# S5's angle fractions on GpSimd instead of VectorE, and another order of VectorE's steps at the end of bc's first half

## What is computed

```
lam_bar = jnp.exp(lam * dt)
bu = jnp.einsum("gpc,blgc->blgp", b_bar, ug.astype(jnp.complex64))
_, states = lax.associative_scan(_lin_rec, (a_el, bu), axis=1)
y = jnp.einsum("gcp,blgp->blgc", cmat, states).real + d_skip * ug
```

## Time and profile before

| | before |
|---|---|
| time, median of 3 runs | 1672.93 us (1672.84 to 1673.79) |
| the profiled execution: time, span | 1673.03 us, 1671.3 us |
| PE busy | 1661.6 us (99%) |
| DVE busy | 1315.7 us (79%) |
| ACT busy | 984.2 us (59%) |
| POOL busy | 234.9 us (14%) |
| granted clock of PE, mean | 0.999 |

### The profile page before, as it was taken

The page is one execution under the profiler, slowest core; times in us unless marked ns, Lnnn a source line. Parts: engine busy times, 40 slices in busy tenths (PEclk is TensorE's granted clock), DMA queues, the critical chain, the costliest instruction groups (busy, mean ns, idle before and its releaser), DMA issues.

```text
span 1671.3 us, 24189 instructions
## 1 busy us (share of the span) xinstructions
PE 1661.6 (99%) x8216; PEld 1386.3 (83%) x8216; DVE 1315.7 (79%) x1723; ACT 984.2 (59%) x1365; POOL 234.9 (14%) x337
## 2 busy tenths in 40 slices
PE   9999999999999999999999999999999999999998
PEld 8888888888888888888888888888888888888886
DVE  7999999999999996545766868888878888845544
ACT  7676676666677877444547754444444454454554
POOL 7843342221111110000000200000000000000001
PEclk9999999999999999999999999999999999999999
DMA  7666766666857666666787577777777777766564
GB/s 255 214 196 197 207 202 202 191 196 180 248 201 252 218 223 205 197 192 208 243 254 223 176 233 241 237 245 243 243 244 242 243 233 243 232 190 198 191 189 127
DMA packets 182873, 361.61 MB, mean 216 GB/s; under 512 B 17520, under 2 KB 45456, under 8 KB 182672
## 3 DMA queue, kind: packets, MB, share of 16 engines
q1 hardware_dynamic: 169264, 340.23, 64.0%
q0 software_dynamic: 12336, 19.92, 5.1%
q10 hardware_dynamic: 1200, 0.53, 0.1%
HBM read 335.41 MB, written 18.92 MB: 212 GB/s over the span
## 4 chain that ended last, share of the span: by engine, by line
PE 74%; DVE 2%; ACT 1%; issue 0%; DVEq 0%
PE psum L1930 23%; PE psum L1931 23%; PE psum L1932 23%; PE psum L1915 2%; PE psum L1917 1%; PE psum L2051 1%; DVE wlo L1216 1%; PE psum L2052 0%; DVE dec L1566 0%; ACT whi L740 0%; PE psum L2058 0%; PE psum L1966 0%; DVE dec L1562 0%; ACT xtok L949 0%; DVE zx L1629 0%
## 5 line engine op out<-in xcount | busy, mean ns | idle before, releaser
L740 ACT ACTIVATE whi<-raw 128x1024 fp32r<-128x1024 f32 x580 | 612.6, 1058 | 583.2 <-PE psum L1932 472.0
L1216 DVE TENSOR_TENSOR wlo<-raw,whi 128x1024 fp32r<-128x1024 f32 x580 | 708.8, 1228 | 312.6 <-ACT whi L740 305.9
L1915 PE MATMUL psum<-act,whi 128*128 128x512 f32 x1088 | 342.5, 396 | 0.0
L1930 PE MATMUL psum<-whi,nw 128*128 128x512 f32 x704 | 274.1, 389 | 0.0
L1931 PE MATMUL psum<-wlo,nw 128*128 128x512 f32 x704 | 273.9, 389 | 0.0
L1932 PE MATMUL psum<-whi,nw 128*128 128x512 f32 x704 | 273.9, 389 | 0.0
L1917 PEld LDWEIGHTS psum<-act,wlo 128*128 128x128 f32 x1088 | 204.4, 188 | 48.3
L1917 PE MATMUL psum<-act,wlo 128*128 128x256 f32 x1088 | 213.7, 278 | 0.0
L1915 PEld LDWEIGHTS psum<-act,whi 128*128 128x128 f32 x1088 | 165.6, 189 | 3.3 <-issue 3.2
L1932 PEld LDWEIGHTS psum<-whi,nw 128*128 128x128 f32 x704 | 132.1, 188 | 27.6
L1930 PEld LDWEIGHTS psum<-whi,nw 128*128 128x128 f32 x704 | 132.1, 188 | 27.3
(11 more groups left out here) (255 smaller groups left out, 2236.7 us busy)
## 6 DMA issues: line engine op xcount, KB each, us to landing
raw<-in_w_up SPq DMA_DIRECT2D x176, 512.0 KB, 4.8
raw<-in_w_zx SPq DMA_DIRECT2D x96, 512.0 KB, 3.7
raw<-in_w_down SPq DMA_DIRECT2D x88, 512.0 KB, 4.3
raw<-in_w_gate SPq DMA_DIRECT2D x64, 512.0 KB, 5.2
raw<-in_w_proj SPq DMA_DIRECT2D x48, 512.0 KB, 4.4
raw<-in_w_bc SPq DMA_DIRECT2D x32, 512.0 KB, 3.9
raw<-in_w_glu SPq DMA_DIRECT2D x32, 512.0 KB, 4.5
raw<-in_w_out SPq DMA_DIRECT2D x32, 512.0 KB, 4.7
```

What stands on the lines that cost most here:

```text
L740: fn(whi[:, s, :], raw[:, s, :], ACTF.Copy).then_inc(hi_ready, 1)
L1216: V.tensor_tensor(wlo[:, s, :], raw[:, s, :], whi[:, s, :], ALU.subtract).then_inc(lo_ready, 1)
L1915: mm(psum[:, b + t, :], whi[:, s, cols(t)], x, start=first, stop=False)
L1930: mm(banks[:, t, :], x_hi, high[:, k], start=first and k == 0, stop=False)
```

## The change

In blocks 1 to 7 POOL makes the fractions, with two instructions each (TENSOR_SCALAR, TENSOR_TENSOR) and a wait between them. DVE keeps those of block 0 (`if start`). POOL's other steps in these turns are put in order around them: the filling of output weights is first in a turn, the first fraction stands ahead of `load_next`, the folds and the step sizes (now `dt_rows`) stand behind the second fraction, and the last fraction of a turn, that of the next block's tile 0, behind the third state sum.

In the last group of bc's first half DVE's order becomes: scan, turn on, the group's sums, the state sum, and then the third low part, which stood between the scan and the turn on.

```diff
             horner_steps((11, 9))
             state_sums(0)
-            fill_next(0)
-            load_next(1)
-            fold(2, 2)
-            state_sums(1)
-            fill_next(1)
-            load_next(2)
-            fold(4, 4)
-            state_sums(2)
-            fill_next(2)
-            load_next(3)
-            horner_steps((7, 5, 3))
...
-            state_sums(3)
-            fill_next(3)
-            for blk in range(4, 7):
-                load_next(blk)
-                state_sums(blk)
-                fill_next(blk)
-            state_sums(7)
+
+            def fractions(count):
+
+                pool.wait_ge(angm_ready, count)
+                step.done(G.tensor_scalar(angm[:, 1, :], angm[:, 0, :], MAGIC, None, ALU.subtract))
+                G.tensor_tensor(ang[:, 0, :], angm[:, 1, :], ang[:, 0, :], ALU.subtract).then_inc(ang_ready, 1)
+
+            def dt_rows():
+
+                horner_steps((7, 5, 3))
...
+            for blk in range(1, 8):
+                fill_next(blk - 1)
+                fractions(blk * 4 + 2)
+                if blk < 7:
+                    load_next(blk)
+                state_sum(blk, 0)
+                fractions(blk * 4 + 3)
+                if blk in (1, 2):
+                    fold(2 * blk, 2 * blk)
+                if blk == 3:
+                    dt_rows()
+                state_sum(blk, 1)
+                fractions(blk * 4 + 4)
+                state_sum(blk, 2)
+                if blk < 7:
+                    fractions(blk * 4 + 5)
             pool.wait_ge(rot_free, 1)
...
                     group_conv(*before)
+                    ends_first_half = name == "bc" and i == 0 and r == per - 1
                     s5_scan(tile, last)
-                    if not last:
+                    if not last and not ends_first_half:
                         lo(2)
                     cpad_free(*before)
                     s5_turn_on(r)
-                    if r == per - 1 and name == "bc":
+                    if last:
                         last_state_sum(blk)
                     if r == per - 1 and not last:
                         group_sums(name, i, r)
-                    if not last:
+                    if ends_first_half:
+                        last_state_sum(blk)
+                        lo(2)
+                    if start:
                         s5_fractions(blk * 4 + (r + 2))
                     if r == per - 1 and name == "zx":
                         last_state_sum(blk)
```

More of the change, by code:

```diff
@@ L646, in _ @@
             state_sums(0)
-            fill_next(0)
-            load_next(1)
-            fold(2, 2)
-            state_sums(1)
-            fill_next(1)
-            load_next(2)
-            fold(4, 4)
-            state_sums(2)
-            fill_next(2)
-            load_next(3)
-            horner_steps((7, 5, 3))
-            step.done(G.tensor_scalar(series, series, 1.0, 2.0, ALU.add, ALU.mult))
-            mul(series, series, ratio)
-            step.done(G.tensor_scalar(square, dtx[0:DT, :], 0.0, None, ALU.max))
@@ L672, in _ @@
-            state_sums(7)
+            def fractions(count):
[4 more added lines that the diff above has]
+                horner_steps((7, 5, 3))
+                step.done(G.tensor_scalar(series, series, 1.0, 2.0, ALU.add, ALU.mult))
+                mul(series, series, ratio)
+                step.done(G.tensor_scalar(square, dtx[0:DT, :], 0.0, None, ALU.max))
+                mul(dt, series, square, ALU.add)
+                G.tensor_scalar(ratio, dt, dtp[0:DT, 2:3], -1.0, ALU.mult, ALU.mult).then_inc(dt_row, 1)
+                pool.wait_ge(dt_row, 1)
+                for k, at_k in ((0, 0), (1, P)):
+                    pool.dma_start(scr[:, at_k:at_k + P], dtw[64 * k:64 * k + HEADS, 0, :]).then_inc(scr_w, 16)
```

## The result

| | before | after |
|---|---|---|
| time, median | 1673.04 us (1672.63 to 1674.09) | 1675.82 us (1675.5 to 1676.54) |
| ratio, 95% interval | | 1.0016 (1.0010 to 1.0022) |
| the profiled execution: span | 1671.3 us | 1674.5 us |

The changed kernel takes 2.78 us more. The time lies inside the prediction's range, but the forecast change of 1.41 us is half of the measured one. The interval of the ratio lies above 1, and the shortest time after (1675.5 us) lies above the longest before (1674.09), so the kernel is slower, by 0.16%. The 3.35 us that the prediction took for the least that can be told from no change were too coarse a measure.

What follows compares the result with a forecast made beforehand. PE bounds the kernel, with DVE's gapless bc queue just behind: 7 x 0.52 - 6 x 0.33 = 1.66 us, less the lead of 0.25, gives 1.41 us more, a median of 1674.3 us; range 1672.4 to 1676.6.

Steps and rivals of the forecast that it cites:

- What bounds the kernel: Mixer: PE sets the pace; DVE is just ahead in zx turns, behind in bc, where its gains and losses add up.
- the lead of 0.25 us: Late in bc's second half: DVE has a low part ready at most 0.25 us before PE begins its unit at 425.98.
- Removed from DVE: bc, 344.30 to 424.53: six fractions of 0.33 us leave DVE's queue, 1.98 us in all.
- The price on DVE: POOL's pair beside DVE's SBUF instructions: 0.42 + 0.10 = 0.52 us a fraction, seven fractions in bc.
- The upper bound of 0.84: Most that one POOL fraction could cost DVE: 2 x 0.42 = 0.84 us.
- The signs: bc: DVE's steps and low parts 0.1 to 0.42 us longer, tiles about 0.2; PE's late low-part waits 1 to 2 us.
- Rival (b): DVE stands still for POOL's whole instruction: 1.61 us a fraction, 1682 us; chance 0.09, including any price above 0.8.
- Rival (a): DVE and POOL hardly meet: 0.25 us or less a fraction, PE's 0.41 wait gone, 1672.5 us; chance 0.27.
- POOL's queue at nothing: POOL's queue, blocks 1 to 7: some 1.8 us a tile fits in POOL's room and costs nothing.
- the spare 1.2 us: Block 3, the tightest place: POOL's fraction done at 235.3, ACT reads it at 236.56.
- The end of bc's first half: New order could remove PE's 0.41 us wait, but DVE is 1.09 us later, so most of this gain goes again.
- The zx turns: 0.76 us a turn falls into DVE's 2.5 us of slack and costs nothing.

Runs made afterwards that it cites:

- experiment 3: Changed kernel with the fractions of blocks 1 to 7 made on neither engine and ACT not waiting for them: 1672.88 us (ratio 0.9999).
- experiment 2: Kernel before with only DVE's new order at the end of bc's first half, DVE still making the fractions: 1673.28 us (ratio 1.0002).
- experiment 5: Changed kernel with ACT making the next tile's angles ahead of a high part, so POOL's pair comes earlier: 1673.46 us (ratio 1.0001).
- Experiment 7: Changed kernel with POOL's pair of instructions made twice in every tile: 1689.37 us (ratio 1.0096).
- experiment 1: Changed kernel with DVE's old order at the end of bc's first half, POOL still making the fractions: 1675.88 us (ratio 1.0017).
- Experiment 6: Changed kernel with POOL making only the fractions of blocks 1 to 5 and DVE those of bc, new order kept: 1673.43 us (ratio 1.0002).
- experiment 4: Changed kernel with POOL doing the TENSOR_SCALAR only, the subtraction of the angle left out: 1672.83 us (ratio 0.9999).
- experiment 8: Changed kernel with POOL's pair made twice for the seven fractions of bc alone: 1680.0 us (ratio 1.0040).

## Why the prediction was right, step by step

**What bounds the kernel**: right. PE is on time up to bc, and what DVE loses in bc arrives at PE, but for the lead of 0.25 us.

**Removed from DVE**, 0.33 us a tile: right (0.34 in experiment 3).

**The price on DVE** was the deciding term and was mis-sized: 0.52 forecast, 0.63 measured. The two-input part was near (0.42 against 0.49), the one-input part of 0.10 came from the copy of the earlier trace rows and measured 0.14. That row was a weak source: the copy takes 0.59 us in the changed kernel where nothing holds it (302.29), so in its 1.27 it was waiting itself, and the low part there takes 1.31 us in the changed kernel too (299.24), where the copy comes 3 us later; what gave its 0.11 isn't shown. With 0.63 the sum is 7 x 0.63 - 1.98 - 0.25 = 2.18 us; PE was 2.32 late at that unit, where 1.41 was forecast. Row by row it closes better: six pairs at 0.63, the one of block 7's tile 0 at 0.55 (a low part of 1.77 us for 1.22), and 0.19 for the new order (experiment 2), which the forecast had at nothing: 3.78 + 0.55 + 0.19 - 1.98 - 0.25 = 2.29. The upper bound of 0.84 held. So the mechanism and the form of the sum were right, and its main term was a sixth too small. Of the 1.37 us by which the forecast change fell short 0.91 arose up to this unit; the rest lies behind it and is mostly not assigned.

**The signs.** The steps grew by 0.63 us, more than the 0.1 to 0.42 named, and a tile by 0.29 for about 0.2. PE's wait for a low part late in the second half was 0.89, for 1 to 2: the other part was paid earlier, at 391 and 399.

**Rival (b)**, DVE blocked for POOL's whole instruction: falls as the price of a fraction. POOL's pair takes 1.58 + 0.74 us in that tile and DVE loses 0.63, of which 0.14 to the first. For a two-input instruction that begins first it is nearer than the forecast had it: the turn back of experiment 5 lost 0.58 us to one of 0.74. And it holds for POOL's side: POOL's first instruction waits, 1.58 against 0.86 us, for about what is left of the low part. The Trainium skill's rule (SBUF — State Buffer, SBUF: two separate sides) that the shared pair is a lock and no split of bandwidth agrees with these rows as far as the one that begins second waits (358.78 and 395.31 in experiment 5, POOL beside the low parts); that it is blocked for the whole instruction is not what DVE's 0.14 us beside the one-input instruction shows. **Rival (a)**, no meeting, is what experiment 5 builds for four of seven pairs, so the condition was sound; the input's arrival at 370.95 was read rightly as lying in the all-SBUF steps.

**POOL's queue at nothing**: right in the sum, with a step that failed. I gave the pair its undisturbed 1.8 us. In block 3 the pairs took 2.7 (217.97 to 220.65) and 2.8, and the spare 1.2 us was gone:

```profile
233.78 1.60 POOL L651 TENSOR_SCALAR angm<-angm 128x256 f32<-128x256 f32 x1
235.47 1.13 POOL L652 TENSOR_TENSOR ang<-angm,ang 128x256 f32<-128x256 f32 x1
...
236.69 0.42 ACT L840 ACTIVATE ang<-ang 128x256 f32<-128x256 f32 x1 [0.15 <-POOL ang L652]
```

ACT waited 0.15 us, at no cost. Experiment 7 shows what stands behind that edge. I had priced the meeting for DVE only and not for POOL.

**The end of bc's first half**: I wrote that most of the 0.41 goes again; all of it went, and 0.65 was lost. With 0.63 for 0.52 the forecast's own working gives it: 4 x 0.63 - 0.99 = 1.53 us later, so the state sum is done at 391.45 and PE starts at 391.82; they were 391.53 and 391.68. A wait that I hadn't named follows: `ub` (S5's output, read by PE at 399.19) starts at 398.50 instead of 396.56, for 0.62 us of PE. DVE's rows, and the POOL instruction beside them:

```profile
396.81 1.77 DVE L1225 TENSOR_TENSOR wlo<-raw,whi 128x1024 fp32r<-128x1024 f32 x1
398.50 0.47 DVE L1431 SCALAR_TENSOR_TENSOR ub<-ub,parm,psum 128x256 f32<-128x256 f32 x1
...
396.21 1.28 POOL L652 TENSOR_TENSOR ang<-angm,ang 128x256 f32<-128x256 f32 x1
```

The 1.94 us are the 1.39 by which DVE is late at the rotation ahead (394.95 for 393.56: four pairs less four fractions, and the order's 0.19) and 0.55 in this low part. In experiment 1, with the old order, `ub` is nearly as late (398.16), but PE, held up for 1.89 us before, comes there later still and doesn't wait; the time is the same. So the reorder lets PE through at 391 only to meet the same lateness at 399, and the wait for the last low parts swallows either.

**The zx turns**: right. DVE's busy time in the turn of the earlier trace rows rose from 44.46 to 45.67 us; ahead of the rotation at 297 its idle time fell from 1.03 to 0.51 us, and PE stayed busy throughout. Experiment 6 says the same.

## What to carry to other kernels

Before work goes from VectorE to GpSimd, look at what VectorE does at the moment when the input arrives: beside instructions with two SBUF inputs the move can cost more (0.63 us) than it saves (0.33), beside instructions fed from PSUM it cost nothing in experiment 5. Count both sides, since GpSimd's own instruction grows as well, and with it the time at which its result is ready. Where VectorE stands without a gap over a stretch, an order that takes one wait away gives it back at the next; the stretch's last wait is the one to count up to.

## What was not expected of the hardware

GpSimd can lose more than VectorE when they meet: in bc a 128x256 TENSOR_SCALAR rose from 0.86 to as much as 1.70 us, while VectorE lost 0.14 us to it in experiment 4. Where it began inside a low part of bc, its growth was what was left of that low part, so the moment of arrival set it. And TensorE's granted clock fell to 0.50 behind pauses of 2.41 and 1.94 us in experiment 7, which cost 1.7 us each time in addition to the pause, and not behind another of 1.94 us in experiment 8; what else differs there is open.
